# The conditioning's sums over partitions: VectorE turns them in 32 by 32 blocks and TensorE joins them in five groups, with the attention's matmuls, its tail and the last stores reordered

## What is computed

```
mod = silu(c) @ w_ada + b_ada              # (1, 9 * 2048): sh1 sc1 gt1 sh2 sc2 gt2 sh3 sc3 gt3
h = rmsnorm(x, g1) * (1 + sc1) + sh1
x = x + 0.5 * gt1 * rmsnorm(swiglu(h, w1_gate, w1_up, w1_down), g1_post)
h = rmsnorm(x, g2) * (1 + sc2) + sh2
x = x + gt2 * rmsnorm(mixer(h), g2_post)   # mixer: w_in, 8 latent and 8 forgetting heads, w_o
h = rmsnorm(x, g3) * (1 + sc3) + sh3
x = x + 0.5 * gt3 * rmsnorm(swiglu(h, w2_gate, w2_up, w2_down), g3_post)
```

## Time and profile before

| what | us |
|---|---|
| median of three runs | 1900.13 |
| lowest and highest run | 1894.65, 1901.73 |
| the profiled execution's own time | 1898.13 |
| its span in the trace | 1896.4 |
| TensorE busy | 1865.0 |
| VectorE busy | 1343.2 |
| ScalarE busy | 895.3 |

### The profile page before, as it was taken

The page is one execution under the profiler, slowest core; times in us unless marked ns, Lnnn a source line. Parts: engine busy times, 40 slices in busy tenths (PEclk is TensorE's granted clock), DMA queues, the critical chain, the costliest instruction groups (busy, mean ns, idle before and its releaser), DMA issues.

```text
span 1896.4 us, 24767 instructions
## 1 busy us (share of the span) xinstructions
PE 1865.0 (98%) x9088; PEld 1570.8 (83%) x9088; DVE 1343.2 (71%) x1601; ACT 895.3 (47%) x1145; POOL 0.2 (0%) x4
## 2 busy tenths in 40 slices
PE   7999999999999999999999999999999999999998
PEld 6888888888887788899988788888888888888886
DVE  4998877788888888689876778877544545444444
ACT  4688644344444333654446446444444444434443
POOL 0000000000000000000000000000000000000000
PEclk9999999999999999999999999999999999999999
DMA  9998888899989988578992585888666666555553
GB/s 377 400 372 276 260 269 276 284 331 326 330 298 337 340 307 307 198 243 289 333 308 73 186 302 163 309 285 285 213 190 189 192 190 190 172 194 193 195 190 132
DMA packets 264763, 488.46 MB, mean 258 GB/s; under 512 B 21606, under 2 KB 32220, under 8 KB 264412
## 3 DMA queue, kind: packets, MB, share of 16 engines
q1 hardware_dynamic: 263792, 486.67, 76.3%
q10 hardware_dynamic: 876, 0.53, 0.1%
HBM read 485.04 MB, written 2.10 MB: 257 GB/s over the span
## 4 chain that ended last, share of the span: by engine, by line
PE 90%; DVE 4%; DMA 2%; DVEq 2%; ACT 1%; issue 1%; SPq 0%; ACTq 0%
PE pair L1463 27%; PE pair L1465 27%; PE pair L1464 27%; PE tps L1546 2%; PE pair L1512 2%; PE pair L1515 2%; PE pair L1514 2%; DVE start_acc L967 1%; DMA start_raw<-in_w_ada 1%; DMA raw<-in_w_down 1%; DVEq L966 1%; DVE w_lo L935 1%; PE mps L1584 1%; DVE acc L954 1%; PE mps L1620 1%
## 5 line engine op out<-in xcount | busy, mean ns | idle before, releaser
L576 ACT ACTIVATE w_hi<-raw 128x1024 fp32r<-128x1024 f32 x634 | 667.9, 1056 | 888.8 <-PE pair L1465 470.7
L935 DVE TENSOR_TENSOR w_lo<-raw,w_hi 128x1024 fp32r<-128x1024 f32 x634 | 770.2, 1218 | 407.2 <-ACT w_hi L576 402.1
L1463 PE MATMUL pair<-w_hi,h_hi 128*128 128x512 f32 (+1 forms) x1656 | 647.3, 391 | 2.5 <-DVE w_lo L935 2.5
L1465 PE MATMUL pair<-w_hi,h_lo 128*128 128x512 f32 (+1 forms) x1656 | 642.9, 388 | 0.0
L1464 PE MATMUL pair<-w_lo,h_hi 128*128 128x512 f32 (+1 forms) x1656 | 642.1, 388 | 0.0
L1463 PEld LDWEIGHTS pair<-w_hi,h_hi 128*128 128x128 f32 x1656 | 311.2, 188 | 65.3 <-issue 3.4
L1465 PEld LDWEIGHTS pair<-w_hi,h_lo 128*128 128x128 f32 x1656 | 311.0, 188 | 64.1
L1464 PEld LDWEIGHTS pair<-w_lo,h_hi 128*128 128x128 f32 x1656 | 311.4, 188 | 61.8
L954 DVE SCALAR_TENSOR_TENSOR acc<-raw,c_col,acc 128x512 f32<-128x512 f32 x420 | 315.7, 752 | 44.2 <-DMA raw<-in_w_ada 10.0
L1463 PE MATMUL pair<-w_hi,hid_hi 128*128 128x512 f32 x704 | 276.2, 392 | 1.2 <-DVE w_lo L935 0.9
L1465 PE MATMUL pair<-w_hi,hid_lo 128*128 128x512 f32 x704 | 274.2, 390 | 0.0
(11 more groups left out here) (208 smaller groups left out, 890.4 us busy)
## 6 DMA issues: line engine op xcount, KB each, us to landing
raw<-in_w_ada SPq DMA_DIRECT2D x224, 512.0 KB, 4.8
raw<-in_w_gate SPq DMA_DIRECT2D x176, 512.0 KB, 4.2
raw<-in_w_up SPq DMA_DIRECT2D x176, 512.0 KB, 3.9
raw<-in_w_down SPq DMA_DIRECT2D x176, 512.0 KB, 4.0
start_raw<-in_w_ada SPq DMA_DIRECT2D x64, 512.0 KB, 7.5
raw<-in_w_in SPq DMA_DIRECT2D x56, 512.0 KB, 4.7
raw<-in_w_o SPq DMA_DIRECT2D x32, 512.0 KB, 5.1
raw<-in_w_uq SPq DMA_DIRECT2D x12, 256.0 KB, 4.4
```

What stands on the lines that cost most here:

```text
L576: nc.scalar.activation(w_hi[:, w % HI_RING, :, 0:n], raw[:, r % RING, :, 0:n], ACT.Copy).then_inc(hi_ready, 1)
L935: nc.vector.tensor_tensor(w_lo[:, r % RING, :, 0:n], raw[:, r % RING, :, 0:n], w_hi[:, w % HI_RING, :, 0:n], ALU.subtract).then_inc(raw_us ...
L1463: nc.tensor.matmul(o, hi, wh, start=first and kk == 0, stop=False, skip_group_check=added)
L1465: ins = nc.tensor.matmul(o, lo, wh, start=False, stop=last and kk == 1, skip_group_check=added)
```

## The change

After the last A unit of a quarter, VectorE itself turns `acc` in 32 by 32 blocks (`transpose`, into the second half of `acc`) and reduces the result to 16 numbers per partition, in `part_sum`, with two more drains. What is left is a sum over the four groups of 32 partitions. TensorE does it for a group of quarters at once: four products with `gather`, a constant of zeros and ones of 128 by 128 each, with 16 or 32 columns moving. There are five groups (quarters 8 to 11, 12 to 19, 20 to 23, 24 to 31, 32 to 35), summed after block 7 of gu1, after blocks 0 and 2 of down1, after block 2 of `wo` and after block 4 of gu2; VectorE adds the bias later, in one instruction per group that reads PSUM. All the old transposes, reductions and their waits go. `gather` is made at the start (a memset and four small reductions).

The four A units of the first block of `wo` move from behind units 5, 6, 7 and 7 to behind units 1, 2, 3 and 4, that is, among the last heads; their loads move in the ring with them. The score's products are issued by kind instead of by tile: first all f32 products of both tiles, then the bf16 ones. At the very end the second tile is added and stored in four pieces of 512 columns instead of two of 1024.

```diff
--- before.py
+++ after.py
@@ -69,6 +69,9 @@
 OPEN = 8
 OPEN_FF = OPEN // 2
 
+GROUPS = [(8, 12, 0), (12, 20, 4), (20, 24, 0), (24, 32, 4), (32, 36, 0)]
...
-    pl["wo"] = [Block(at, pattern(8, after), 1, wo_q)
-                for after in ([5, 6, 7, 7], [1, 3, 4, 5, 6, 7], [1, 3, 4, 5, 6, 7], [])]
+    pl["wo"] = [Block(at, pattern(8, after), 1)
+                for after in ([1, 2, 3, 4], [1, 3, 4, 5, 6, 7], [1, 3, 4, 5, 6, 7], [])]
...
+        part_sum = sb("part_sum", [P, 12 * 4 * DB])
...
+        gather = sb("gather", [P, DB, P])
...
-            for n in range(4):
-                t, c = n // 2, slice(n % 2 * XB, (n % 2 + 1) * XB)
+            for n in range(2 + DB):
+                t, c = (0, slice(n * XB, (n + 1) * XB)) if n < 2 else (1, slice((n - 2) * NB, (n - 1) * NB))
                 sp.wait_ge(x_ready, 4 * 2 + n + 1)
                 sp.dma_start(out[t * P:(t + 1) * P, c], x[:, t, c]).then_inc(out_stored, 16)
-            sp.wait_ge(out_stored, 16 * 4)
+            sp.wait_ge(out_stored, 16 * (2 + DB))
...
                 ins.then_inc(raw_used, 1)
+                if j0 == 7:
+                    first, _, base = next(g for g in GROUPS if g[0] <= q < g[1])
+                    dve.drain()
+                    nc.vector.transpose(acc[:, 1, :], acc[:, 0, :])
+                    dve.drain()
+                    at = bass.ds(plus((base + q - first) * 4 * DB, i, 4 * DB if per else 0), 4 * DB)
+                    nc.vector.tensor_reduce(part_sum[:, at], acc[:, 1, :].rearrange("p (b j) -> p b j", j=32), AX_X,
+                                            ALU.add).then_inc(part_ready, 1)
...
-            def mod_columns(b, i=0, per_q=0):
-
-                k, c0 = DB * len(b.sums), plus(DB * b.sums[0], i, DB * per_q)
-                dve.wait_ge(sum_ready, plus(b.m + 1, i, int(per_q > 0)))
-                for j in range(len(b.sums)):
-                    nc.vector.tensor_reduce(ada_sum[:, j * DB:(j + 1) * DB],
-                                            mps[:, j, :].rearrange("p (c k) -> p c k", c=DB), AX_X, ALU.add)
-                dve.drain()
-                nc.vector.tensor_tensor(mod[:, bass.ds(c0, k)], ada_sum[:, 0:k], col[:, bass.ds(c0, k)],
-                                        ALU.add).then_inc(mod_ready, 1)
+            def mod_columns(g):
+
+                first, end, _ = GROUPS[g]
+                c = slice(DB * first, DB * end)
+                dve.wait_ge(sum_ready, g + 1)
+                nc.vector.tensor_tensor(mod[:, c], mps[:, 0, 0:DB * (end - first)], col[:, c], ALU.add).then_inc(mod_ready, 1)
...
-                    for h in range(2):
-                        c = slice(h * XB, (h + 1) * XB)
+
+                    width = XB if following is not None or t == 0 else NB
+                    for h in range(D // width):
+                        c = slice(h * width, (h + 1) * width)
...
+            nc.vector.memset(gather[:], 0.0)
             dve.drain()
             dve.wait_ge(c_ready, 1)
             def small_tiles():
 
                 dve.wait_ge(small_landed, SMALL)
                 nc.vector.tensor_copy(msk[:, 0, :], ident)
+                for q in range(DB):
+
+                    nc.vector.tensor_reduce(gather[:, q, 32 * q:32 * q + 32], ident.rearrange("p (g i) -> p i g", i=32), AX_X, ALU.add)
...
-                            if before.sums and (b.sums or count == 1):
-                                mod_columns(before, i, 1)
...
+                dve.drain()
+                mod_columns(0 if f == "1" else 4)
                 dve.drain()
                 gate_columns(pre_v + 2, G_POST["ffn" + f], 0.5)
                 lo_unit(b0, 0)
                 lo_unit(b0, 1)
                 hidden(last)
-                if f == "1":
-                    mod_columns(last)
...
-                            if pl[down][n - 1].sums:
-                                mod_columns(pl[down][n - 1])
+                            if f == "1" and n in (1, 3):
+                                mod_columns(n // 2 + 1)
...
-                        lo_unit(wo[0], n - N_ATT)
-                lo_unit(wo[0], 4)
+                        run(wo[0], start=n - N_ATT, stop=n - N_ATT + 1)
+                run(wo[0], start=4, stop=5)
                 for n, b in enumerate(wo):
                     tasks = {}
                     if n:
-                        if wo[n - 1].sums:
-                            tasks[3] = lambda ada=wo[n - 1]: mod_columns(ada)
+                        if n == 3:
+                            tasks[3] = lambda: mod_columns(3)
...
-            def sum_columns(b, i=0, per=0, per_m=0):
-
-                pe.wait_ge(raw_used, plus(b.r_sums(), i, per))
-                if per_m or b.m:
-                    pe.wait_ge(mod_ready, plus(b.m, i, per_m))
-                for k in range(DB * len(b.sums)):
-                    c = slice((k % 4) * P, (k % 4 + 1) * P)
-
-                    ins = nc.tensor.transpose(mps[:, k // 4, c], acc[:, b.slots[k // 4], c], ident)
+            def sum_columns(g):
+
+                first, end, base = GROUPS[g]
+                pe.wait_ge(part_ready, end - GROUPS[0][0])
+                if g:
+                    pe.wait_ge(mod_ready, g)
+                rows = part_sum[:, 4 * DB * base:4 * DB * (base + end - first)].rearrange("p (k q) -> p k q", q=DB)
+                for q in range(DB):
+                    ins = nc.tensor.matmul(mps[:, 0, 0:DB * (end - first)], gather[:, q, :], rows[:, :, q],
+                                           start=q == 0, stop=q == DB - 1)
...
-                        if b.sums:
-                            sum_columns(b, i, len(b.seq), 1)
+                    if start == (FB - 4 if f == "1" else 4):
+                        sum_columns(0 if f == "1" else 4)
...
-                    if b.sums:
-                        sum_columns(b)
+                    if f == "1" and n in (0, 2):
+                        sum_columns(n // 2 + 1)
...
-                pe.wait_ge(mod_ready, pl["win"][-1].m + 1)
...
                     for t in range(TT):
-                        q = slice(t * P, (t + 1) * P)
-                        keys = slice(0, (t + 1) * P)
-                        o = bank[:, P * t:P * t + (t + 1) * P]
-                        diagonal = bank[:, P * t + t * P:P * t + (t + 1) * P]
-                        if n < HEADS:
-                            nc.tensor.matmul(o, fqk[:, n, q], fqk[:, HEADS + n, keys], start=True, stop=False)
-                            nc.tensor.matmul(diagonal, msk[:, 0, :], msk[:, 1, :], start=False, stop=False)
-
-
-                            ins = nc.tensor.matmul(o, sel_b[:, n, :], cumT[:, keys], start=False, stop=True)
-                        else:
-                            h = n - HEADS
-                            nc.tensor.matmul(o, qnT[:, h, q], knT[:, h, keys], start=True, stop=False)
-                            nc.tensor.matmul(diagonal, msk[:, 0, :], msk[:, 2, :], start=False, stop=False)
-                            ins = nc.tensor.matmul(o, qrT[:, h // 2, q], krT[:, h % 2, keys], start=False, stop=True)
+                        q, keys = slice(t * P, (t + 1) * P), slice(0, (t + 1) * P)
+                        tiles.append((t == 0, q, keys, bank[:, P * t:P * t + (t + 1) * P],
+                                      bank[:, P * t + t * P:P * t + (t + 1) * P]))
+
+                    if n < HEADS:
+                        for first, q, keys, o, _ in tiles:
+                            nc.tensor.matmul(o, fqk[:, n, q], fqk[:, HEADS + n, keys], start=first, stop=False, skip_group_check=True)
+                        for _, _, _, _, diagonal in tiles:
+                            nc.tensor.matmul(diagonal, msk[:, 0, :], msk[:, 1, :], start=False, stop=False, skip_group_check=True)
+                        for _, _, keys, o, _ in tiles:
+                            ins = nc.tensor.matmul(o, sel_b[:, n, :], cumT[:, keys], start=False, stop=True, skip_group_check=True)
+                    else:
+                        h = n - HEADS
+                        for first, q, keys, o, _ in tiles:
+                            nc.tensor.matmul(o, qnT[:, h, q], knT[:, h, keys], start=first, stop=False, skip_group_check=True)
+                            nc.tensor.matmul(o, qrT[:, h // 2, q], krT[:, h % 2, keys], start=False, stop=False, skip_group_check=True)
+                        for _, _, _, _, diagonal in tiles:
+                            ins = nc.tensor.matmul(diagonal, msk[:, 0, :], msk[:, 2, :], start=False, stop=True, skip_group_check=True)
...
+                    if n == 2:
+                        sum_columns(3)
```

More of the change, by code:

```diff
@@ L91, with __init__ @@
 class Block:
[L98 to L99 removed]
+    def __init__(self, at, seq, products):
+        self.r, self.w, self.a, self.g = at["r"], at["w"], at["a"], at["g"]
         self.seq = seq
@@ L107, in __init__ @@
         at["g"] += products
[L108 to L113, removed]
     def r_of(self, u):
         return self.r + self.seq.index(("W", u))
```

(22 more changed lines are left out.)

19 lines of the change are left out of this document (6 added, 13 removed).

## The result

The changed kernel takes 1907.53 us (median of 11 runs, 1904.13 to 1911.66), the kernel before 1898.17 on the same chip (11 runs): a ratio of 1.0047, interval 1.0036 to 1.0057. That is slower by 9 us, where 3.6 us faster was forecast, and 11.0 above the forecast 1896.5, outside its range of 1888 to 1904. The profiled execution has a span of 1907.1 us where the one before has 1896.4.

A forecast was written before the change was run, and what follows sets the result against it. TensorE was taken to set the pace, with next to no lead for VectorE in down1's A part. Cost 8.5 less gains 12.1 gave -3.6 us, so 1896.5 us, range 1888 to 1904.

The forecast's parts named there:

- The cost: TensorE's added waits for VectorE behind quarter ends, mostly in down1: 8.5 us, ends 0 and 11.9.
- The insertions: VectorE's added turn and reduction with drains at each of 28 quarter ends: 1.5 us each, ends 1.3 and 2.1.
- The reading: Lead of the next `w_lo` at 28 quarter ends in the old trace: 12 show waits, together 11.9 us.
- The relief: Taken off the 11.9 us: 1.9 for waits already there outside `wo`, 1.5 for saturated loads catching up.
- The gains: Sums on TensorE 9.0, scores 1.3, moved A units 1.2, last stores 0.6: together 12.1 us.
- all of it lies on TensorE's path: The 14.0 us of removed sums count in full for TensorE, since VectorE was never late for them.
- Scores and moved units: In the heads, f32 products before bf16 save 1.3 us; in `wo`, moved A units remove a 1.2 us wait.
- The last stores: At the very end, pieces of half the size start earlier: 0.6 us saved, ends 0 and 1.0.
- VectorE's price, slower: Rival: turn costs a 1024-column pass, insertion 2.1 us, waits 21.5 at 18 ends, mainly down1 and `win`: 1909.5; chance 0.11.
- Dear products: Rival: the five groups' products on TensorE cost twice a transpose, 4.4 us less gain, 1900.9; chance 0.12.
- The cover holds: Rival: the load ring and four `w_hi` slots absorb the insertions, cost at most 1.5 us, 1888.0 to 1889.5; chance 0.27.

The follow-up runs named there:

- e1: Changed kernel without VectorE's turn and reduction at the 28 quarter ends, a one-column memset in their place: 1890.14 us, ratio 0.9961 to the kernel before.
- e11: Changed kernel with turn and reduction moved some units later for down1's quarters 18 to 24 alone, sums in two alternating slots: 1898.41 us, ratio 1.0003 to the kernel before.
- e2b: Kernel before with turn and reduction added at each of the 28 quarter ends, their spare buffers behind all others: 1913.67 us, ratio 1.0074.
- e7: Kernel before with one transpose instead of 4 or 8 in each of down1's four sums, 24 fewer: 1895.03 us, ratio 0.9986.
- e5: Changed kernel with each turn and reduction 2 to 8 units later, two slots, groups 1 to 3 a block later: 1888.38 us, ratio 0.9951 to the kernel before.
- e8: Kernel before with one unused buffer of 64 bytes in each partition behind `acc`: 1939.47 us, ratio 1.0214.
- e9: Kernel before with one unused buffer of 128 bytes in each partition behind `acc`: 1933.59 us, ratio 1.0191.
- e2: Kernel before with turn and reduction added at each of the 28 quarter ends, their spare buffers right behind `acc`: 1950.11 us, ratio 1.0278.
- e12: Kernel before with one unused buffer of 512 bytes in each partition behind `acc`: 1898.71 us, ratio 1.0004.
- e10: e5 with 384 unused bytes ahead of all weights: 1894.11 us, ratio 0.9973 to the kernel before.
- e4: Changed kernel with the turn of each quarter done twice: 1931.08 us, ratio 1.0164 to the kernel before.
- e3: Kernel before with only the score's product order, the four moved A units and the last stores in smaller pieces: 1894.42 us, ratio 0.9978.

## Why the prediction was wrong

**The cost.** This is the step that failed: "At 16 of them nothing shows. At 12 it does" (of the 28 ends), "together 11.9 us", less relief ("3.4 - 1.5 = 1.9 us [...] need not come on top" and "where TensorE slips, the saturated loads [...] catch up, for which I take another 1.5"), to 8.5 us. The insertions cost 17.3. By stage, the changed kernel against e1, one execution each, in us:

| stage | read, without relief | measured |
|---|---|---|
| gu1 | 0.7 | 3.9 |
| down1 | 8.8 | 9.7 |
| projections | 2.4 | 3.0 |
| `wo` and FFN 2 | 0 | 0.6 |

**Leads that were not there.** The largest error is in gu1. The reading went by "its next `w_lo`" alone and by the trace of the kernel before. Behind quarter 8 `hidden` stands first: 1.3 us against e1. Quarter 14 ends with its block, and its next `w_lo` is wanted by the next block's first product. In the kernel before it was ready at 448.89 and used at 450.68, a lead of 1.8 us, of which TensorE spent 0.8 on the eight transposes that the change takes away. The changed kernel waits 1.45 us there, at 451.95, and e11 the same; e2b, which keeps the transposes, doesn't wait there, and e1, which has no insertion, doesn't either. So a gain took the cover that the insertion needed. Waits of PE, 380 to 550 us, the changed kernel, then e1:
```profile
PE pair L1458 <- DVE w_lo L925: 1.6, 2, 1.4
PE tps L1541 <- DVE s L1103: 1.0, 1, 1.0
```
```profile
PE tps L1538 <- DVE s L1099: 0.3, 1, 0.3
```

**The relief.** It can't be taken off the reading's total. In e2b, where nothing else changes, down1 lost 8.5 us, and the reading without relief had 8.8. But this agreement is partly luck, as two errors cancel. Waits of PE in down1 (555 to 800 us), before and e2b:
```profile
PE pair L1463 <- DVE w_lo L935: 0.9, 3, 0.6
```
```profile
PE pair L1470 <- DVE w_lo L937: 9.4, 7, 1.4
```
By distances between starts, e2b's seven waits cost 1.5 to 1.7 us each, 11.3 together: the whole insertion and 0.11 for the product behind it, where the reading had 0.81 to 1.41. Against that, the waits that were there before (2.1 with their restarts) are gone, as predicted, and some 0.7 is caught up. The catching up can't be laid on the loads: DMA moved less in down1, not more. Stretches of down1, before and after:
```profile
560.00:620.00 60.00, 59.72 (x264) 47.75 (x263) 50.37 (x58) 24.44 (x26) 0.00 (x0) 1.00 0.92 325
```
```profile
560.00:620.00 60.00, 57.06 (x252) 45.83 (x251) 49.07 (x57) 22.84 (x25) 0.00 (x0) 1.00 0.90 318
```

**What a wait costs.** The reading gave how much later a product starts. The product behind it comes late too, by 0.08 to 0.11 us, which makes some 1.2 us for 12 stalls. Whoever sums recorded waits has to add 0.27 for each.

**The gains.** The prices were right where TensorE runs on: of the four blocks of FFN 2 behind a quarter's end three are 0.49 to 0.52 us shorter in the changed kernel (predicted 0.52; in e1 all four), and the one with a group's four products 0.97 longer than without (predicted 1.0). What failed was "all of it lies on TensorE's path": with no insertion at all (e1) 7.3 us of the 12.1 arrive. This is the second failed step, and with 4.8 us no small one beside the cost's 8.8. In gu1, the heads, `wo` and FFN 2 nearly all arrives; by the table some 2.1 us are missing in down1 and 2.5 in the projections, where VectorE is hardly ahead. A TensorE that is spared work runs into the next `w_lo` sooner: in these two stages e1 waits for it 3.2 us in 8 waits on record, where the kernel before has 1.2 in 5. With their restarts that is 2.8 of the 4.6 us, and 1.5 of it is the one wait in block 5 of `w_in` that some executions have and others not. The rest is open. In e7, which saves only 2.7, all of it arrives. Scores and moved units were right together (2.5), and the wait of 1.2 us in `wo` is gone. The last stores, 0.6 predicted, gave 0: the additions end 0.25 us later behind TensorE's last product (four pieces in 2.74 us, two were 2.48) and that takes up what the smaller last piece saves.

**The rivals.** "VectorE's price, slower" had the sign and nearly the time (1909.5), but not the mechanism: it wanted an insertion of 2.1 us, and it is 1.48. It put the break-even at "an insertion of 1.5", with waits equal to the gains; at 1.48 the insertions cost 17.3 and the gains were 7.3. The Trainium skill ("VectorE: DVE Perf Modes", Rules for kernel authors) advises few chained operations and leaves a transpose of 128 by 128 to TensorE where PSUM will do. This kernel agrees with it only by half: with the same chained operations at another place (e5) it is 9 us ahead. "Dear products" is refuted (0.97 a group). Eight records take 0.81 us, from 1388.19 to 1389.00, 0.10 each, near the 0.11 that was taken. The Trainium skill's gap of 25 ns for 1 to 64 columns ("TensorE: Matmul & The Clock Gate", Back-to-back issue gap) doesn't price these products; the measurement decides. "The cover holds" is refuted by 9 waits in down1.

The chances were 0.07 for slower by over 0.5%. At +0.47% the result is just below that bound, with the interval's ends on either side of it.

## What to carry to other kernels

Before an operation is inserted on an engine that runs close ahead of another, list everything queued behind it that the other engine waits for, not the most frequent kind alone. Read each lead as it will be once the rest of the change is in, not as it is in the old trace: work taken off the waiting engine shortens it. Take each missing lead at full price with the restart on top, and count on no catching up without a measured one. Then ask for the place: 1.5 us at 28 ends cost 17 us at the quarter's end and next to nothing a few units later, where no other extra work stood ahead of TensorE's next operand.

## What the runs showed of the hardware, unexpected

**A buffer's place.** 64 unused bytes slowed TensorE's f32 products by 6 ns each and the kernel by 2.1%. Slow were the kernels in which the stationary tiles (`h_hi`, `hid_hi`) were moved against the moving ones (`w_hi`, `w_lo`) by 64, 128 and 2112 bytes (e8, e9, e2). Fast are a distance moved by 512 bytes (e12), and kernels in which all moved together, by 768 (changed, e5) and 1152 (e10). That fits the distance between the two operands and not the stationary tile's own address: moved by 128 alone it is slow, moved by 1152 (128 more than 1024) with the moving ones it is fast. It holds for the products with 512 moving columns. Those of `w_in` that have `w` as the stationary operand and 256 columns were not slower (records of 279 ns in e8 and 281 in e9, 283 before). 256 bytes was not tried, and why it is so stays open. Anyone who adds a buffer for an experiment should put it last.

**The clock behind a wait.** Waits up to 1.4 us in the changed kernel, and those up to 2.0 in e4, left the granted clock at 1.00; behind waits of 2.1 to 2.2 us in e4 (four of six), 2.4 in e3 and 3.0 in e10 its mean fell to 0.94, 0.90 and 0.87 of 2.4 GHz in the stretch around them, so TensorE ran at 1.2 GHz for a part of it. That cost 7.2 us beside 17.2 of waits in e4's down1. Beside the single waits of e3 and e10, 2.7 and 3.2 us with their restarts, it cost 1.3 and 1.4 (4.0 - 2.7, 4.6 - 3.2), or 1.7 by the clock granted from 905 to 925 us.
